# Hybrid encoder trunk: the first feed-forward part's down projection regrouped into products of 512 and 256 columns

## The reference, cut to what matters

```python
def swiglu(h, w_gate, w_up, w_down):
    return (jax.nn.silu(h @ w_gate) * (h @ w_up)) @ w_down
...
    for l in range(DEPTH):
        x = x + 0.5 * swiglu(rmsnorm(x, ffn1_norm[l]), ffn1_w_gate[l], ffn1_w_up[l], ffn1_w_down[l])
        h = rmsnorm(x, mix_norm[l])
        proj = (h @ w_in[l]).astype(f32)
...
        x = x + y @ w_out[l]
        x = x + 0.5 * swiglu(rmsnorm(x, ffn2_norm[l]), ffn2_w_gate[l], ffn2_w_up[l], ffn2_w_down[l])
    return rmsnorm(x, final_norm)
```

## Time and profile before

| | |
|---|---|
| median of two runs | 1926.78 us (1925.85 to 1927.71) |
| profiled execution, first to last instruction (span) | 1927.2 us |
| granted TensorE clock, mean of the span | 0.999 |
| busy: PE, PEld | 1919.3 us, 1579.1 us |
| busy: DVE, ACT, POOL | 754.3, 701.8, 904.0 us |
| read from HBM | 178.45 MB, 94 GB/s |

### The profile page before, as it was taken

The page is one execution under the profiler, slowest core; times in us unless marked ns, Lnnn a source line. Parts: engine busy times, 40 slices in busy tenths (PEclk is TensorE's granted clock), DMA queues, the critical chain, the costliest instruction groups (busy, mean ns, idle before and its releaser), DMA issues.

```text
span 1927.2 us, 28344 instructions
## 1 busy us (share of the span) xinstructions
PE 1919.3 (100%) x10396; PEld 1579.1 (82%) x10396; DVE 754.3 (39%) x1209; ACT 701.8 (36%) x975; POOL 904.0 (47%) x550
## 2 busy tenths in 40 slices
PE   9999999999999999999999999999999999999999
PEld 7888888788788888888888888887878888888887
DVE  6222221389875322231132222214898752222312
ACT  5222222365643322222332222324556432222223
POOL 3444444466335544444444444444654444444443
PEclk9999999999999999999999999999999999999999
DMA  5332333322213333333323333332222223333332
GB/s 182 104 99 90 96 97 99 99 67 89 67 55 99 109 98 98 97 90 100 103 93 98 99 91 93 97 100 89 78 79 75 66 91 108 98 98 95 91 100 97
DMA packets 53504, 181.84 MB, mean 94 GB/s; under 512 B 6816, under 2 KB 6816, under 8 KB 53408
## 3 DMA queue, kind: packets, MB, share of 16 engines
q1 hardware_dynamic: 53264, 180.56, 30.1%
q10 hardware_dynamic: 144, 0.00, 0.0%
HBM read 178.45 MB, written 2.10 MB: 94 GB/s over the span
## 4 chain that ended last, share of the span: by engine, by line
PE 99%; DMA 0%; ACT 0%; DVE 0%; issue 0%; SPq 0%; ACTq 0%
PE ps L1467 31%; PE ps L1469 31%; PE ps L1468 31%; PE ps L1685 1%; PE ps L1602 1%; PE ps L1604 1%; PE ps L1603 1%; PE ps L1733 0%; PE ps L1799 0%; PE ps L1963 0%; PE ps L1746 0%; PE ps L1804 0%; DMA x<-in_x 0%; PE ps L1487 0%; PE ps L1783 0%; PE ps L1717 0%
## 5 line engine op out<-in xcount | busy, mean ns | idle before, releaser
L481 POOL TENSOR_TENSOR wlo<-raw,whi 128x1024 fp32r<-128x1024 f32 (+1 forms) x536 | 901.7, 1698 | 1015.2 <-ACT whi L542 553.6
L1467 PE MATMUL ps<-hhi,whi 128*128 128x512 f32 x1760 | 691.6, 393 | 2.2 <-DVE hlo L848 1.7
L1469 PE MATMUL ps<-hhi,wlo 128*128 128x512 f32 x1760 | 686.5, 390 | 0.0
L1468 PE MATMUL ps<-hlo,whi 128*128 128x512 f32 x1760 | 686.3, 390 | 0.0
L1467 PEld LDWEIGHTS ps<-hhi,whi 128*128 128x128 f32 x1760 | 330.9, 188 | 76.1 <-issue 4.1
L1469 PEld LDWEIGHTS ps<-hhi,wlo 128*128 128x128 f32 x1760 | 330.9, 188 | 69.6
L1468 PEld LDWEIGHTS ps<-hlo,whi 128*128 128x128 f32 x1760 | 331.0, 188 | 67.4
L1469 PE MATMUL ps<-ahi,wlo 128*128 128x512 f32 x704 | 274.1, 389 | 0.0
L1467 PE MATMUL ps<-ahi,whi 128*128 128x512 f32 x704 | 274.1, 389 | 0.0
L1468 PE MATMUL ps<-alo,whi 128*128 128x512 f32 x704 | 274.1, 389 | 0.0
L536 ACT ACTIVATE whi<-raw 128x1024 fp32r<-128x1024 f32 x168 | 177.2, 1055 | 265.3 <-PE ps L1469 246.0
(11 more groups left out here) (276 smaller groups left out, 1354.6 us busy)
## 6 DMA issues: line engine op xcount, KB each, us to landing
raw<-in_up SPq DMA_DIRECT2D x168, 512.0 KB, 3.4
raw<-in_mix SPq DMA_DIRECT2D x64, 512.0 KB, 3.4
raw<-in_dn SPq DMA_DIRECT2D x64, 448.0 KB, 3.3
raw<-in_dn SPq DMA_DIRECT2D x32, 512.0 KB, 3.5
raw<-in_lead SPq DMA_DIRECT2D x8, 512.0 KB, 3.5
x<-in_x SPq DMA_DIRECT2D x8, 256.0 KB, 6.2
raw<-in_lead SPq DMA_DIRECT2D x8, 256.0 KB, 6.3
raw<-in_mix SPq DMA_DIRECT2D x8, 256.0 KB, 2.5
```

The costliest lines, as they stand in the source:

```text
L481: low = pool.tensor_tensor(wlo[:, q, part], raw[:, q, part], whi[:, q, part].bitcast(F32), ALU.subtract)
L1467: mm(dst, whi[:, q, s], mh, start=start, stop=False)
L1468: mm(dst, whi[:, q, s], ml, start=False, stop=False)
L1469: return mm(dst, wlo[:, q, s], mh, start=False, stop=stop)
```

## The change

In the part c = 0, `ahi` and `alo` become the two halves of one tile `aboth`, at the same addresses as before. For each block of weights and each half t of the tokens (256 tokens), one matmul of 512 columns takes the high weights times [high half, low half] and writes the two results side by side into one bank; a second, of 256 columns, adds low weights times the high half to the bank's first half. The two token halves have a bank each, banks 4 and 5 for even m and 1 and 2 for odd m. DVE then adds the four quarters to x, in four instructions of 256 columns, with a wait for its own first two ahead of the third (both write the same columns of x). The part c = 1 stays as it was.

```diff
-        ahi = place("ahi", [P, NJ, T], 0, F32R)
-        alo = place("alo", [P, NJ, T], 44, F32R)
+        aboth = place("aboth", [P, 2, NJ, T], 0, F32R)
+        ahi, alo = aboth[:, 0], aboth[:, 1]
...
+        HALVES = ((4, 5), (1, 2))
...
-                            return stt(x[:, m, :], bank(DOWN + m % 2), 0.5, x[:, m, :], ALU.mult, ALU.add)
+                            if c == 1:
+                                return stt(x[:, m, :], bank(DOWN + m % 2), 0.5, x[:, m, :], ALU.mult, ALU.add)
+                            pieces = [(part, t) for part in range(2) for t in range(2)]
+                            for part, t in pieces:
+                                cols = slice(t * T // 2, (t + 1) * T // 2)
+                                if part == 1 and t == 0:
+                                    settle()
+                                ins = stt(x[:, m, cols], bank(HALVES[m % 2][t])[:, part * T // 2:(part + 1) * T // 2],
+                                          0.5, x[:, m, cols], ALU.mult, ALU.add)
+                                if (part, t) != pieces[-1]:
+                                    did(ins)
+                            return ins
...
+            def half_products(parity, q, piece, both, start, stop):
+
+                s = slice(piece * P, piece * P + P)
+                for t in range(2):
+                    dst, cols = bank(HALVES[parity][t]), slice(t * T // 2, (t + 1) * T // 2)
+                    mm(dst.rearrange("p (a t) -> p a t", a=2), whi[:, q, s], both[:, :, cols], start=start, stop=False,
+                       skip_group_check=True)
+                    last = mm(dst[:, 0:T // 2], wlo[:, q, s], both[:, 0, cols], start=False, stop=stop,
+                              skip_group_check=True)
+                return last
...
-                                    last = products(bank(DOWN + mm4 % 2), w % NS, j - j0,
-                                                    (ahi[:, j, :], alo[:, j, :]), j == 0, j == NJ - 1)
+                                    if c == 0:
+                                        last = half_products(mm4 % 2, w % NS, j - j0, aboth[:, :, j, :],
+                                                             j == 0, j == NJ - 1)
+                                    else:
+                                        last = products(bank(DOWN + mm4 % 2), w % NS, j - j0,
+                                                        (ahi[:, j, :], alo[:, j, :]), j == 0, j == NJ - 1)
```

More of the change, by code:

```diff
@@ L105 @@
          + [x for p in range(NP) for x in (("cv", p), ("z", p))] + [("g", 1), ("g", 2), ("g", 3)])
-DVE_STEPS = 161
+DVE_STEPS = 185
 CONVS = ["B", "C", 0, 1, 2, 3]
```

## The result

The changed kernel takes 1944.03 us (median of 1943.93 and 1944.12) against 1926.78: 17.25 us longer, a ratio of 1.009 with a 95% interval of 1.006 to 1.0119. That is less than 2%, but clear of noise, and above the forecast range (1924 to 1941).

The account below looks back on a forecast made before the run. The prediction took PE, busy throughout, as the bound: 1927.2 + 2.6 (products) + 1.4 (update of x) = 1931.2 us for the profiled span, and 0.4 less, 1930.8 us, for the median. Range: 1924 to 1941 us.

Parts of the forecast that it names:

- the slow rival: Down projection: the short product cannot hide the next weight load; 1980.8 us, 2.8% slower; chance 6% together with a similar case.
- changing banks is free: Down projection: switching the target bank after every second matmul was taken to cost zero, at most one excess of 13.3 ns.
- the tail: Behind tile 7 in each layer: DVE's four updates of x end 1.01 us later, delaying PE's transposes; 1.4 us in all.
- The 117 ns behind a short product: Down projection: assumed distance from a 256-column product's start to the next start, the middle of 113.3 and 120 ns.
- two accounts: The 13.3 ns excess of a matmul belongs to its columns (113.3 ns per short product) or to each matmul with its load (120).
- a triple costs 2 x 226.7 + 2q: Down projection: two long products keep 226.7 ns each, two short ones take q each, against 3 x 226.7 before.
- the term of 2.6 us: PE's products in the down projection: 7.3 ns more for each of 352 triples.
- The seam rival: Down projection: reading the long operand from two places costs 13.3 ns per product, 9.4 us on top, 1940.2 us; chance 14%.
- some 240 ns behind each long one: Sign in the changed profile's down projection: such a distance after each long product's start would show that two-place reading costs.
- The bound that was set for the stretch, 126 us: First part's down projection to the mixer's first matmul: 121 us expected; the forecast fails over 126 or under 117.
- q = 120: Down projection: a short product takes 106.7 + 13.3 ns if each matmul with its load carries the excess; costs 4.7 us.

Follow-up runs that it names:

- e7: Kernel before with every product of the first part's down projection made as two of 256 columns; 1942.40 us in a single run.
- e1: Kernel before with only the first part's low-weights product halved, one short product after each long one; 1944.64 us against 1928.41, ratio 1.0088.
- e2: Changed kernel with the high and low halves side by side in memory, so the long product reads 512 columns in a row; 1946.49 us, ratio 1.0095.
- e3: Changed kernel with the low-weights product whole, 512 columns in a third bank; 1929.38 us in a single run against a median of 1928.41.
- e5: Kernel before with a seventh group of up products written out in layer 0, same matmuls; 1941.17 us against 1927.09, ratio 1.0079.
- e4: Changed kernel with one written-out group of up products in layer 0 left to the loop; 1942.30 us, ratio 1.0072.
- e8: Changed kernel with five written-out groups of up products in layer 0 and seven in layer 1; 1938.10 us against 1927.09, ratio 1.0056.
- e6: Kernel before with the first part's low-weights product halved, in the order long, long, short, short; 1940.25 us in a single run.
- e11: Kernel before with the first part's low products halved, all long products of each weight piece before its short ones; 1943.76 us against 1926.81, single runs.
- e9: Kernel before with the first part's down projection using only 64 of each 128 weight columns, half its outputs left out; 1929.96 us, single run.

## Why the prediction was wrong

Right were: that PE alone sets the time; that the load is not exposed (the slow rival; in e7 at most 13.3 ns of it show behind 256 columns, even in a row); that changing banks is free (e1, all in one bank, has the same stretch); and the tail, 1.2 us against 1.4 (the pieces took 420 ns, not 457). The 117 ns behind a short product were met in part by luck: they were the middle between two accounts, and neither gives them. In an even row a short product takes 120.0 ns (e7); beside long ones 113, 117 and 120 ns follow one another, 117.0 in the mean. Two steps failed.

The first is the formula "a triple costs 2 x 226.7 + 2q". It let the long product keep the distance that it has in an even row. Beside short products it has 236.3, so the term of 2.6 us was 9.4: 352 x (2 x 236.3 + 2 x 117.0 - 680.0) = 9.4 us. The seam rival named a price of about this size for the long product (13.3 ns, measured 9.6), and the sign given for it, some 240 ns behind each long one, came; but its mechanism is false: e2 and e3 show that the seam costs nothing, and e1 that the alternation alone costs all of it. The bound that was set for the stretch, 126 us, was too wide to catch it. How the time splits: 4.7 us are the fourth matmul's own 13.3 ns, the end of the range that was given for q = 120 (e7), and 4.7 us come from mixing sizes.

The second is a term that the sum does not have: the 88 matmuls of written-out code more in layer 0. They were counted as time on PE and not as code that moves everything behind it. In the mixer of layer 0 PE stood 4.3 us more than before and lost some 2.3 us more around the pauses, 1.6 of them at the lower clock behind the first; 7.15 less the 0.6 of the tail, 6.5 us, is the cost. e5 shows that moved code alone does this to the kernel before, and e4 and e8 that other places take away more than half of it (e4) or three quarters (e8). The rows read for the prediction gave no sign of it: before the change the mixer had less than 0.1 us of such pauses, which says that the code happened to lie well, not that the place does not matter.

Together: 9.4 + 6.5 + 1.2 for the tails of both layers + 0.1 for a short pause in layer 1 = 17.2 us of the 17.25 measured.

What stays open is why a mixed row costs more than its matmuls do in even rows. Beyond 13.3 ns each, a block costs 13.3 ns more in long-short order (e1), 3.3 in pairs (e6), 2.6 in sorted pieces (e11) and none when all are alike (e7, before). Open too is why the clock falls behind some pauses and not behind others of the same length.

None of these versions beats the kernel before. e3 comes nearest with its three matmuls of 512 columns a block, and it shows what the regrouping needed: the high product may read two halves at no cost, as long as the low product stays whole.

## What to carry to other kernels

On a kernel that is bound by PE, count matmuls as well as columns: each one costs a fixed 13.3 ns here beside its columns, and a row in which long and short ones alternate costs more than either in an even row. Written-out code has a place as well as a length: a change that adds instructions moves all the code behind it, and bursts of small matmuls may then wait microseconds for their instructions and run on at the lower clock. So look for PE waits marked "issue" in stages that the change did not touch, and try another place before judging the change itself.

## What the runs showed that was not expected

Moving code alone cost 14 us of 1927 (e5), nearly as much as the whole change. Of the 16 pauses of over 1.5 us without a releaser in these mixers, 10 were followed by 3 us or more at the level of 1.2 GHz and 6 were not. With the slow stretch a pause costs up to 2.6 times its own length (e5: 1.96 us idle, 5.1 us in all), without it little more than its length (2.44 and 2.7 us in the changed kernel). Reading an operand of 512 columns from two places 44 KB apart is free (e3). Loads of half the width made a matmul not faster but 3.3 ns slower (e9).
